# Last down projection part of the feed-forward in two passes over the tokens, with the second layer norm of finished token groups placed between the second pass's matmuls

## The reference, cut to what matters

```
h2 = x * (1 + scale2) + shift2
g_ff, u_ff = split(h2 @ ffn_w_gu)              # 1024 -> 2 x 2816
f = (silu(g_ff) * u_ff) @ ffn_w_down           # 2816 -> 1024
x = layer_norm(ALPHA * x + gate2 * f, ln2_g, ln2_b)
```

## Time and profile before

| | |
|---|---|
| time of the program, median of 3 runs | 4011.57 us (4010.5 to 4011.73) |
| the profiled execution: its own time | 3996.53 us |
| its span, first to last instruction | 3994.4 us |
| TensorE matmul busy | 3487.3 us, 87% |
| TensorE weight loads busy | 2975.3 us, 74% |
| VectorE busy | 1563.1 us, 39% |
| ScalarE busy | 1122.4 us, 28% |
| mean granted TensorE clock, whole span | 0.924 |

### The profile page before, as it was taken

How to read it: one execution, slowest core, us unless ns; L and a number is a source line. 1 busy time by engine, 2 the same in 40 slices (tenths; PEclk the granted TensorE clock), 3 DMA queues, 4 the chain that set the end, 5 groups by cost and what they waited for, 6 DMA issues and landing times. The chain is left out here.

```text
span 3994.4 us, 53828 instructions
## 1 busy us (share of the span) xinstructions
PE 3487.3 (87%) x22344; PEld 2975.3 (74%) x22344; DVE 1563.1 (39%) x3034; ACT 1122.4 (28%) x2096; POOL 168.7 (4%) x240
## 2 busy tenths in 40 slices
PE   2984869899888999999969476899999799999997
PEld 1772436666778999999958343566669699999997
DVE  3225556544433222222341445664443423232324
ACT  3122145444322111111141222563431411112113
POOL 0000011111000000000000100201100000000000
PEclk8996779999899999999989677999999899999998
DMA  4012410244101111111111052005421011111111
GB/s 157 38 30 99 158 28 1 96 159 159 54 1 49 43 47 42 50 40 51 32 41 32 28 185 76 1 1 190 159 75 42 32 40 51 42 50 39 47 43 56
DMA packets 80880, 255.64 MB, mean 64 GB/s; under 512 B 15436, under 2 KB 30958, under 8 KB 69495
## 3 DMA queue, kind: packets, MB, share of 16 engines
q1 hardware_dynamic: 68054, 164.04, 12.4%
q0 software_dynamic: 11520, 83.89, 5.9%
q10 hardware_dynamic: 1056, 4.19, 0.3%
HBM read 245.59 MB, written 6.51 MB: 63 GB/s over the span
## 5 line engine op out<-in xcount | busy, mean ns | idle before, releaser
L372 PE MATMUL psum<-h_hi,w_ffn_hi 128*128 128x384 f32 (+1 forms) x2112 | 697.5, 330 | 37.5 <-DVE w_ffn_lo L1969 37.5
L374 PE MATMUL psum<-h_hi,w_ffn_lo 128*128 128x384 f32 (+1 forms) x2112 | 694.6, 329 | 0.0
L373 PE MATMUL psum<-h_lo,w_ffn_hi 128*128 128x384 f32 (+1 forms) x2112 | 684.7, 324 | 0.0
L372 PEld LDWEIGHTS psum<-h_hi,w_ffn_hi 128*128 128x128 f32 x2112 | 397.6, 188 | 37.8 <-DVE w_ffn_lo L1969 37.8
L373 PEld LDWEIGHTS psum<-h_lo,w_ffn_hi 128*128 128x128 f32 x2112 | 397.5, 188 | 0.0
L374 PEld LDWEIGHTS psum<-h_hi,w_ffn_lo 128*128 128x128 f32 x2112 | 396.6, 188 | 0.0
L374 PE MATMUL psum<-ffn_act_hi,w_ffn_lo 128*128 128x384 f32 (+1 forms) x1056 | 344.7, 326 | 0.0
L373 PE MATMUL psum<-ffn_act_lo,w_ffn_hi 128*128 128x384 f32 (+1 forms) x1056 | 344.4, 326 | 0.0
L372 PE MATMUL psum<-ffn_act_hi,w_ffn_hi 128*128 128x384 f32 (+1 forms) x1056 | 344.1, 326 | 0.0
L358 DVE SCALAR_TENSOR_TENSOR xT<-psum,adaT,xT 128x384 f32<-128x384 f32 (+1 forms) x240 | 136.6, 573 | 419.0 <-PE psum L374 419.0
L1985 DVE TENSOR_TENSOR ffn_act<-silu_tmp,psum 128x384 f32<-128x384 f32 x132 | 70.3, 533 | 562.7 <-PE psum L374 562.7
(11 more groups left out here) (369 smaller groups left out, 5880.8 us busy)
## 6 DMA issues: line engine op xcount, KB each, us to landing
w_ada_pair<-in_w_ada SPq DMA_DIRECT2D x48, 1024.0 KB, 5.0
w_ffn<-in_w_gu SPq DMA_DIRECT2D x88, 512.0 KB, 3.5
w_ffn<-in_w_down SPq DMA_DIRECT2D x32, 384.0 KB, 3.2
w_ffn<-in_w_down SPq DMA_DIRECT2D x32, 320.0 KB, 2.9
w_out<-in_w_out SPq DMA_DIRECT2D x16, 512.0 KB, 6.9
w_in_T<-in_w_in_T SPq DMA_DIRECT2D x12, 512.0 KB, 4.4
z<-in_x_prompt SPq DMA_DIRECT2D x1, 4096.0 KB
w_ada_first<-in_w_ada SPq DMA_DIRECT2D x2, 2048.0 KB, 17.3
```

The costliest lines, as they stand in the source:

```text
L372: pe.matmul(o, wh, xh, start=first, stop=False)
L373: pe.matmul(o, wh, xl, start=False, stop=False)
L374: return pe.matmul(o, wl, xh, start=False, stop=last)
```

## The change

- The eight "d" pieces of the last part become sixteen: first c = 0 to 7 with token groups 0 and 1, then c = 0 to 7 again with group 2 alone. The weights of the second eight are loaded and split again. From here the matmuls use banks 0 to 3 only; banks 4 to 7 go to the norm.
- The second layer norm leaves ln_back and becomes `group_norm`, worked in steps (group, step) inside stage_ffn. Steps 0 to 2 turn one block each to rows, 1 to 3 norm them, 4 to 7 bring two chunks each back, and after the last of these the group is modulated into HT. `beside[j]` names the steps that follow the j-th group of matmuls of the second pass, `behind` those that follow all matmuls: group 1 from step 4, and all of group 2.
- All three engines take the same steps in the same places of their order; the samples are modulated last.

The diff, cut to its core (`stats`, `scale`, `root` and `norm` hold the same instructions and waits as those in `ln_rows`, with the block's pair of banks from `rows_psum`):

```diff
+        def group_norm(name, zr, g_col, b_col, sh, sc, added):
...
+            def rows_psum(blk):
+                return bank(4 + 2 * (blk % 3 % 2), 2)
+
+            def turn(pe, blk):
+                n, g = rows(blk), blk // 3
+                if blk % 3 == 0:
+                    added(pe, g)
+                    if g:
+                        pe.wait_ge(ea, 4 * g)
+                        pe.wait_ge(ed, 4 * g)
+                if blk % 3 == 2:
+                    pe.wait_ge(nm, blk - 1)
+                for c in range(KD):
+                    ins = pe.transpose(rows_psum(blk)[0:n, c * P:c * P + P], XT[:, c, blk * P:blk * P + n], ident)
+                ins.then_inc(tr, 1)
+
+            def back(pe, g, c):
+                t0, w = GROUPS[g]
+                if c == 0:
+                    pe.wait_ge(nm, 3 * g + 3)
+                if c >= 4:
+                    pe.wait_ge(xt[c % 2], 4 * g + (c - 4) // 2 + 1)
+                for blk in range(3 * g, 3 * g + 3):
+                    r = rows(blk)
+                    ins = pe.transpose(bank(4 + c % 4)[:, blk * P - t0:blk * P - t0 + r], zr[0:r, blk % nz, c * P:c * P + P],
+                                       CST[0:r, C_ID:C_ID + r])
+                ins.then_inc(tb, 1)
...
+            def keep(eng, par, g, c):
+                t0, w = GROUPS[g]
+                eng.wait_ge(tb, KD * g + c + 1)
+                affine(eng, XT[:, c, t0:t0 + w], bank(4 + c % 4)[:, 0:w], PRM[:, g_col + c:g_col + c + 1],
+                       PRM[:, b_col + c:b_col + c + 1]).then_inc(xt[par], 1)
+                if c < KD - 2:
+                    return
+                wp = min(t0 + w, TP) - t0
+                eng.wait_ge(xt[par], 4 * g + 4)
+                for k in range(par, KD, 2):
+                    affine(eng, HT[:, k, t0:t0 + wp], XT[:, k, t0:t0 + wp], ADA[:, sc + k, 0:1], ADA[:, sh + k, 0:1])
+
+            def on_pe(pe, g, step):
+                if step < 3:
+                    turn(pe, 3 * g + step)
+                elif step >= 4:
+                    for c in (2 * (step - 4), 2 * (step - 4) + 1):
+                        back(pe, g, c)
+
+            def on_act(act, g, step):
+                if g == 0 and step == 4:
+                    act.wait_ge(xd, 1)
+                if step < 3:
+                    root(act, 3 * g + step)
+                if 1 <= step <= 3:
+                    norm(act, 3 * g + step - 1)
+                if step >= 4:
+                    keep(act, 0, g, 2 * (step - 4))
+
+            def on_dve(dve, lk, g, step):
+                if step < 3:
+                    stats(dve, lk, 3 * g + step)
+                if 1 <= step <= 3:
+                    scale(dve, lk, 3 * g + step - 1)
+                if step >= 4:
+                    keep(dve, 1, g, 2 * (step - 4) + 1)
...
+        ZF = at("ln2_rows", r1, [P, 8, D])
 
         def stage_ffn():
...
-                    pieces += [("g", f, f0, KD), ("u", f, f0, KD)]
-                pieces += [("d", c, f0, f1 - f0) for c in range(KD)]
+                    pieces += [("g", f, f0, KD, (0, 1, 2)), ("u", f, f0, KD, (0, 1, 2))]
+                for ns in ((0, 1, 2),) if f1 < NF else ((0, 1), (2,)):
+                    pieces += [("d", c, f0, f1 - f0, ns) for c in range(KD)]
             NPC = len(pieces)
-            gg = [(i, n) for i in range(NPC) for n in range(3)]
+            gg = [(i, n) for i in range(NPC) for n in pieces[i][4]]
+            ends = [sum(len(p[4]) for p in pieces[:i + 1]) for i in range(NPC)]
+            LAST = len(gg) - KD
+            earlier = (len(PARTS) - 1) * 3 * KD
+
+            def added(eng, n):
+                eng.wait_ge(s_dv, earlier + (3 if n == 2 else 2) * KD)
+            ln_pe, ln_act, ln_dve, ln_params, ln_samples = group_norm("ln2", ZF, Q_LN2G, Q_LN2B, M_SH1, M_SC1, added)
+            beside = [[(0, 0), (0, 1)], [(0, 2)], [(0, 3)], [(0, 4), (0, 5)], [(0, 6), (0, 7)], [(1, 0), (1, 1)], [(1, 2)],
+                      [(1, 3)]]
+            behind = [(1, step) for step in range(4, 8)] + [(2, step) for step in range(8)]
+            home = [bank(g % 8 if g < LAST else g % 4) for g in range(len(gg))]
...
                         if i >= NSW:
-                            sp.wait_ge(s_mm, 3 * (i - NSW + 1))
+                            sp.wait_ge(s_mm, ends[i - NSW])
...
                         ins.then_inc(s_mm, 1)
+                        if g >= LAST:
+                            for step in beside[g - LAST]:
+                                ln_pe(pe, *step)
+                    for step in behind:
+                        ln_pe(pe, *step)
+
+                def order(split, group, ln):
 
                     split(0)
                     split(1)
                     for g, (i, n) in enumerate(gg):
                         group(g, i, n)
-                        if n == 0 and i + 2 < NPC:
+                        if n == pieces[i][4][0] and i + 2 < NPC:
                             split(i + 2)
+                        if g >= LAST:
+                            for step in beside[g - LAST]:
+                                ln(*step)
+                    for step in behind:
+                        ln(*step)
...
                     for k in range(KD):
                         dve.wait_ge(s_hh, k + 1)
                         dve.tensor_tensor(HL[:, k].bitcast(F32R), HT[:, k], HH[:, k], ALU.subtract).then_inc(s_hl, 1)
-                    order(split, group)
+                    order(split, group, lambda n, step: ln_dve(dve, lk, n, step))
+                    ln_samples(dve)
...
             run(stage_ffn)
-            run(ln_back, Q_LN2G, Q_LN2B, XT, "ln2", (M_SH1, M_SC1))
```

More of the change, by code:

```diff
@@ L1886, in stage_ffn @@
                 for f in range(f0, f1):
-                    pieces += [("g", f, f0, KD), ("u", f, f0, KD)]
-                pieces += [("d", c, f0, f1 - f0) for c in range(KD)]
+                    pieces += [("g", f, f0, KD, (0, 1, 2)), ("u", f, f0, KD, (0, 1, 2))]
+                for ns in ((0, 1, 2),) if f1 < NF else ((0, 1), (2,)):
+                    pieces += [("d", c, f0, f1 - f0, ns) for c in range(KD)]
             NPC = len(pieces)
-            gg = [(i, n) for i in range(NPC) for n in range(3)]
+            gg = [(i, n) for i in range(NPC) for n in pieces[i][4]]
[9 more added lines that the diff above has]
+            home = [bank(g % 8 if g < LAST else g % 4) for g in range(len(gg))]
             reader = {"g": s_sl, "u": s_um, "d": s_dv}
             seen, number = {"g": 0, "u": 0, "d": 0}, []
+            updated, due = {}, []
             for i, n in gg:
-                kind = pieces[i][0]
+                kind, c = pieces[i][0:2]
                 seen[kind] += 1
                 number.append((reader[kind], seen[kind]))
+                due.append(updated.get((c, n), 0) if kind == "d" else 0)
+                if kind == "d":
+                    updated[c, n] = seen[kind]
+            free = [None if g < 8 else number[g - 8] for g in range(LAST)]
+            for g in range(LAST, len(gg)):
+                at_bank = g % 4
+                free.append(number[g - 4] if g >= LAST + 4 else number[max(k for k in range(LAST) if k % 8 == at_bank)])
             with nc.Block() as block:
@@ L1900, in _ @@
                 def _(sp):
-                    for i, (kind, c, f0, nk) in enumerate(pieces):
+                    for i, (kind, c, f0, nk, _) in enumerate(pieces):
                         if i >= NSW:
-                            sp.wait_ge(s_mm, 3 * (i - NSW + 1))
+                            sp.wait_ge(s_mm, ends[i - NSW])
                         if kind == "d":
@@ L1913, in _ @@
                     for g, (i, n) in enumerate(gg):
-                        kind, c, f0, nk = pieces[i]
+                        kind, c, f0, nk, ns = pieces[i]
                         t0, w = GROUPS[n]
                         if g >= 8:
-                            pe.wait_ge(*number[g - 8])
-                        if n == 0:
+                            pe.wait_ge(*free[g])
+                        if n == ns[0]:
                             pe.wait_ge(s_wl, i + 1)
@@ L1959, in _ @@
                         act.copy(HH[:, k].bitcast(F32R), HT[:, k]).then_inc(s_hh, 1)
-                    order(split, group)
+                    order(split, group, lambda n, step: ln_act(act, n, step))
                 @block.vector
@@ L1992, in group @@
                             dve.wait_ge(s_mm, g + 1)
[L1993 to L1996, removed]
+                            if due[g]:
+                                dve.wait_ge(s_dv, due[g])
+                            residual(dve, lk, s_dv, TMPF, home[g], c, n, M_G2)
                     for k in range(KD):
```

50 lines of the change are left out of this document (45 added, 5 removed).

## The result

| | before | changed |
|---|---|---|
| median of 8 runs each | 4010.86 us (4006.80 to 4011.95) | 4023.45 us (4018.73 to 4025.11) |
| ratio, with its 95% interval | | 1.0035 [1.0026, 1.0044] |
| the profiled execution: its own time | 3996.53 us | 4018.73 us |
| its span, mean granted clock | 3994.4 us, 0.924 | 4017.0 us, 0.919 |

The account below looks back on a forecast made before the run. The second norm was taken as bound by engines waiting for each other, the down part by TensorE. Overlap +2.6 and lower clock +3.9 us a layer, +13.0 for both, gave 4011.6 + 13.0 = 4024.6 us, range 4020 to 4030.

Parts of the forecast that it names:

- The pass, 34.3 us and 1.5 for the clock: Second pass, first to last matmul: 34.3 us in place of 17.5, stalls 8.0 included; lower clock 1.5 more.
- Turn 2: Eight transposes bringing block 2 to rows in the second pass: wait for norm 0 until 9.2 us, stall 3.1.
- The wait before the first way back, 2.1: Second pass, before group 0's chunks are transposed back: TensorE waits for norm 2 until 16.6 us, stall 2.1.
- The tail, 25.5 us and 2.4 for the clock: From the last matmul to the samples' end: 25.5 us where it was 39.7; lower clock 2.4 more.
- turn 8: Tail, eight transposes bringing block 8 to rows: waits for norm 6, ends at 48.0 us; lower clock costs 0.8.
- The price of a chunk: Bringing one chunk back by 3 transposes on TensorE: estimated at 0.41 us for every chunk.
- the Trainium skill's rule: Transposes do not count as busy for TensorE's clock; the tail would run at the lower clock, +6 us a layer.
- The second load at nothing: Second pass: eight more weight loads, roundings and splits cost nothing, hidden behind other pieces' matmuls and transposes.
- Before, 57.2 us from the same point: Kernel before, from the last group-1 matmul: group-2 work of eight pieces plus the norm take 57.2 us.
- No stalls: Rival: no waits in the second pass, -5.5 us a layer, 4000.6 us; chance 0.11.
- No fall of the clock: Rival: the stalls come but TensorE's clock stays up, +2.6 us a layer, 4016.8 us; chance 0.2.
- At every gap: Rival: the clock falls at every gap and stays down long, +12.9 us a layer, 4037.4 us; chance 0.16.

Follow-up runs that it names:

- experiment 6: Changed kernel with norm ahead of root, reciprocal ahead of statistics, group 2's rows in banks 0 to 3 and its first steps moved earlier: 4008.92 us, ratio 1.0005.
- experiment 4: Changed kernel with extra matmuls that nobody reads put before TensorE's five longest waits: 4012.57 us, ratio 1.0019 to the kernel before.
- experiment 8: Kernel before, with 36 unread transposes ahead of the way back in both norms of each layer: 3998.22 us, ratio 0.9973.
- experiment 5: Changed kernel with norm ahead of root, reciprocal ahead of statistics, and fewer unread filler matmuls before five waits: 4003.81 us, ratio 0.9991.
- Experiment 1: Changed kernel's two passes with second weight loads, but the norm back in its own stage: 4008.22 us, ratio 1.0005 to the kernel before.
- experiment 11: Changed kernel with a step list for each engine, norm ahead of root, group 2's rows in banks 0 to 3, no fillers: 3996.25 us, ratio 0.9965.
- 9: Changed kernel with a step list per engine, norm ahead of root, group 2 in low banks, two unread matmul fillers, the second moved: 3991.25 us, ratio 0.9957.

## Why the prediction was right, and where its terms were not

The forecast of 4024.6 us came within 1.2 us of the median, inside the forecast's own range. It was less exact than that. Its terms add up to 13.0 us for two layers; the stages show 18.5, and whatever else differs between executions brought the medians back to 12.6. That closeness is luck; the direction and the chain of waits are not.

- **The pass, 34.3 us and 1.5 for the clock: 35.8. Measured 35.7 and 35.9.** Turn 2 was to start at 9.2 and did at 3942.00 - 3932.80 = 9.2; the first way back at 16.6, measured 17.2; turn 5 at 31.0, measured 31.4. Two errors cancel. The waits were 2.9, 1.0 and 2.9 us, 6.9 in place of 8.0. The clock already fell behind turn 2, where I had put nothing: it was 0.66 between 3942 and 3946. The two falls cost some 2.5 us (experiment 6 has the same two), against 1.5 in the sum.
- **The wait before the first way back, 2.1: measured 1.0.** The matmuls ahead of it ran at the lower clock, so TensorE came later to a wait that ended at its own time. A slower clock ahead of a wait is partly paid out of the wait: in experiment 6 the same wait was 1.01 us in the layer where the clock had fallen and 1.56 in the other.
- **The tail, 25.5 us and 2.4 for the clock: 27.9. Measured 30.1, both layers.** This is the step that failed, and it is over the 30 us that the prediction set as its own limit. The waits were sized well (2.6, 4.1, 4.4; measured 2.5, 4.0, 4.2). Two terms were mis-sized, and experiment 4 tells them apart: in its layer 1, where the clock stayed at 1.00 to the end, the tail took 26.5 us. So 1.0 us was missing at full clock, and the lower clock took 3.6 where 2.4 were forecast.
  - *The clock.* At turn 8 the forecast 0.8 came (1.91 in place of 1.06). At group 1's way back 1.1 was forecast and none came. At the last way back 0.5 was forecast, on the rule of 3 us at the lower clock behind each long wait, and 2.7 came (7.38 in place of 4.64): from turn 8 on the clock stood at 0.50 to the end of the stage.
  - *The price of a chunk.* 0.41 us is the mean of all 24 chunks. At clock 1.00 a chunk of group 0 or 1 takes 0.33 and one of group 2, with its 64-row transpose, 0.57. So the last way back was priced 1.3 us too low, and each of the others some 0.7 too high; the rest of the 1.0 us lies in small terms.
- **The transposes and the Trainium skill's rule (TensorE: Matmul & The Clock Gate, PE-mode transpose).** It says that transposes do not count as busy in the way that other matmuls do. By it the clock would cost 6 us a layer, an estimate of the prediction's. Pass and tail together lost 6.1 (2.5 and 3.6), nearer to that than to my 3.9, but not in the rule's way: group 1's way back ran at full speed behind a wait of 2.5 us, and in experiment 8 108 transposes with nothing between them but a gap of 0.29 us ran at full speed throughout. So transposes alone can keep the clock up. They don't always: in layer 2 of experiment 4 and layer 1 of experiment 5 the clock fell inside the last way back, 2.7 and 2.6 us after its start, behind waits of 0.65 and 0.62 us. In the other layer of each, with the same instructions, it didn't. The runs fit neither the rule nor its opposite.
- **The second load at nothing.** Experiment 1 found 1.2 to 1.6 us a layer where only matmuls lay between; the change has transposes between, and in its pass TensorE waited for no split. Right within that.
- **Before, 57.2 us from the same point:** the stages agree with it to some 0.5 us. The first pass, taken as unchanged, came out 0.6 and 0.5 us longer.
- **The rivals.** "No stalls" asked for under 5.4 us of waits; there were 6.9. Its price is near what a kernel with few waits reaches: pass and tail come to 51.2 us in experiment 11 and to 50.0 in 9, where 51.7 were worked out, though by other steps and banks than the rival had. "No fall of the clock", 2.6 us a layer, is what experiment 4 tried: it was still 4.5 us a layer over the kernel before, with a fall left in each layer. Its two halves without a fall, the pass of layer 2 (33.7) and the tail of layer 1 (26.5), add to 60.2 us where the forecast without the clock had 59.8. "At every gap" forecast 12.9 a layer; the stages show 9.2.

What stays open: when the clock falls. The same wait of 1.9 us let it fall in one layer and not in the other, and it fell behind 0.65 us too.

## What to carry to other kernels

Work laid beside other work brings only what the order of every engine's queue lets through: in this kernel one and the same overlap cost 0.35% with one list of steps for all engines and gained 0.35% with a list for each engine, the norm ahead of the root and the free banks used. Ask for each step in such a list which older, more urgent result stands behind it on the same engine, and compare the grouped chain by itself (58 us) with the one it replaces (40 us) before counting what the overlap hides. Price instructions by their shape: a mean over unlike chunks (0.41 us) was wrong for both kinds (0.33 and 0.57). A wait of TensorE can be paid twice, in the wait and in the clock behind it; a few matmuls or transposes that nobody reads, released early enough and into a bank that is free, brought 0.27% in a kernel that was otherwise untouched.

## What the runs showed of the hardware that was not expected

- In the changed kernel the granted clock stood at 0.50 from turn 8 to the end of the stage, 18 us, with 7.4 us of transposes without a gap at its end; behind 5.05 us in the kernel before it was back at 1.00 within 10 us. Behind 0.65 us it fell in the middle of transposes in one layer and not in the other (experiment 4), and behind 2.47 us the same 24 transposes took 2.85 us in one kernel and 4.50 in another.
- Behind 1.86 us of waiting the clock fell in layer 1, and behind 1.92 us at the same place in layer 2 it did not: 34.16 and 31.64 us for the same work (experiment 6).
- At clock 1.00 the chunks of a way back start 0.33 us apart; where one of a chunk's three transposes is of the 64-row block, 0.57 us. All 24 transposes take 2.85 and 4.64 us (experiment 4).
- Extra work made the program faster: 36 transposes more in each of four norms took 10.8 us off (experiment 8).
